# A four-layer float32 network on one core: the streamed 256-column tiles are read in another order, in pieces of 64 bytes

## The reference

```python
for layer in range(DEPTH):                      # 2 layers
    mixer = hgrn_gmlp_mixer if layer % 2 == 0 else mla_moba_mixer
    x = x + mixer(x, *mixer_params[layer])
    x = x + peer_ffn(x, *ffn_params[layer])
...
def peer_ffn(x, norm_ffn, w_query, sub_keys, expert_down, expert_up):
    # per token: 8 heads, each the top 16 of 128 x 128 = 16384 experts
    u = jnp.take(expert_down, idx, axis=0)
    act = jax.nn.gelu(jnp.einsum('btd,bthkd->bthk', xi, u))
    v_sel = jnp.take(expert_up, idx, axis=0)
    return jnp.einsum('bthk,bthkd->btd', g * act, v_sel)
```

## Time and profile before

| | |
|---|---|
| time, median of 3 runs | 3422.84 us (3422.46 to 3425.61) |
| the profiled execution's own time | 3413.89 us |
| its span | 3412.2 us |
| PE busy / weight loads busy | 91% / 88% of the span |
| DVE, ACT, POOL busy | 63%, 46%, 18% |
| mean granted TensorE clock | 0.95 of 2.4 GHz |
| matmul records | 25,254 |

### The profile page before, as it was taken

The page is one execution under the profiler, slowest core; times in us unless marked ns, Lnnn a source line. Parts: engine busy times, 40 slices in busy tenths (PEclk is TensorE's granted clock), DMA queues, the critical chain, the costliest instruction groups (busy, mean ns, idle before and its releaser), DMA issues. The chain is left out here.

```text
span 3412.2 us, 66107 instructions
## 1 busy us (share of the span) xinstructions
PE 3119.0 (91%) x25254; PEld 3013.7 (88%) x25254; DVE 2148.7 (63%) x3339; ACT 1571.3 (46%) x2653; POOL 609.7 (18%) x478
## 2 busy tenths in 40 slices
PE   8789999999998588999999997999987699899798
PEld 7689999999997488999999997999975689899697
DVE  4659698789864658888856775332255555454654
ACT  4244566644453444466645454222155244443343
POOL 0119700023321017900022222000010100000000
PEclk9889999999998699999999998999997699999899
DMA  5145544488884134544479893222150145455353
GB/s 173 53 155 172 181 145 143 152 276 299 309 303 124 41 124 161 179 160 144 145 241 314 309 311 132 96 98 93 61 164 11 50 136 185 143 186 163 124 191 123
DMA packets 178899, 560.66 MB, mean 164 GB/s; under 512 B 22480, under 2 KB 31440, under 8 KB 178144
## 3 DMA queue, kind: packets, MB, share of 16 engines
q1 hardware_dynamic: 178784, 559.21, 49.2%
HBM read 558.10 MB, written 1.05 MB: 164 GB/s over the span
## 5 line engine op out<-in xcount | busy, mean ns | idle before, releaser
L228 ACT ACTIVATE peer_e_hi<-peer_raw 128x1024 fp32r<-128x1024 f32 x512 | 539.3, 1054 | 355.6 <-PE peer_e_s L1180 178.0
L232 DVE TENSOR_TENSOR peer_e_lo<-peer_raw,peer_e_hi 128x1024 fp32r<-128x1024 f32 x416 | 516.8, 1244 | 275.9 <-ACT peer_e_hi L228 275.5
L232 DVE TENSOR_TENSOR ffn_lo<-ffn_raw,ffn_hi 128x1024 fp32r<-128x1024 f32 x260 | 318.6, 1227 | 499.9 <-ACT ffn_hi L228 499.9
L228 ACT ACTIVATE ffn_hi<-ffn_raw 128x1024 fp32r<-128x1024 f32 x264 | 279.6, 1061 | 546.0 <-PE ffn_acc L2007 343.1
L1226 PE MATMUL peer_e_o<-x_normed,peer_e_hi 128*128 128x256 f32 x2048 | 482.3, 278 | 13.5 <-ACT peer_e_hi L228 9.9
L1228 PE MATMUL peer_e_o<-x_normed,peer_e_hi 128*128 128x256 f32 x2048 | 481.6, 278 | 0.0
L1226 PEld LDWEIGHTS peer_e_o<-x_normed,peer_e_hi 128*128 128x128 f32 x2048 | 387.0, 189 | 14.3 <-ACT peer_e_hi L228 10.3
L232 POOL TENSOR_TENSOR x_normed<-peer_e_h,x_normed 128x256 fp32r<-128x256 f32 x256 | 207.1, 809 | 1038.1 <-ACT x_normed L228 1038.1
L1228 PEld LDWEIGHTS peer_e_o<-x_normed,peer_e_hi 128*128 128x128 f32 x2048 | 387.2, 189 | 0.0
L1998 PE MATMUL ffn_acc<-x_normed,ffn_hi 128*128 128x256 f32 x1408 | 354.9, 283 | 20.8 <-DVE x_normed L318 18.2
L1999 PE MATMUL ffn_acc<-x_normed,ffn_hi 128*128 128x256 f32 x1408 | 351.3, 281 | 0.0
(11 more groups left out here) (580 smaller groups left out, 7391.1 us busy)
## 6 DMA issues: line engine op xcount, KB each, us to landing
peer_raw<-in_l_down SPq DMA_DIRECT2D x256, 512.0 KB, 3.3
peer_raw<-in_l_up SPq DMA_DIRECT2D x256, 512.0 KB, 4.8
ffn_raw<-in_ffn_wi SPq DMA_DIRECT2D x176, 512.0 KB, 3.5
peer_ring<-in_w_mod SPq DMA_DIRECT2D x144, 512.0 KB, 5.2
ffn_raw<-in_ffn_wo SPq DMA_DIRECT2D x88, 512.0 KB, 3.4
l_in_raw<-in_l_w_in SPq DMA_DIRECT2D x39, 512.0 KB, 3.8
peer_q_raw<-in_l_peer_w_query SPq DMA_DIRECT2D x32, 512.0 KB, 4.0
wg_in_raw<-in_w_in SPq DMA_DIRECT2D x26, 512.0 KB, 4.1
```

Source lines behind the costliest of these rows:

```text
L228: return act.activation(hi, v, ACT.Copy)
L232: return eng.tensor_tensor(lo, v, hi.bitcast(F32), ALU.subtract)
```

## The change

In the four places above the streamed operand and the result get another access pattern over the same 256 elements. `striding` cuts the row into two halves of 128 elements (512 bytes) and each half into 8 pieces of 16 elements (64 bytes), and goes through piece 0 of the first half, piece 0 of the second half, piece 1 of the first, piece 1 of the second, and so on: each piece is followed by the one 512 bytes further. The result is written to PSUM in the same order, so that every element lands where it did. Weights, tiles, their places, waits and all instructions of the other engines stay as they were: each engine's program has as many rows after as before. The operand of each changed matmul goes from 128x256 to 128x8x2x16. The fp32 matmuls, form "t" and the recurrences' matmuls keep their patterns.

```diff
--- before.py
+++ after.py
@@ -92,6 +92,19 @@
     tile = padded(nc, stack, name, shape, dt, LINE)[0]
     stack.enter_context(nc.sbuf_tensor(f"{name}_after", [P, (LINE - MOVED) // 4], F32))
     return tile
+
+
+PIECE = 16
+
+
+def striding(a):
...
+    names = " ".join("abc"[:len(a.shape) - 2])
+    return a.rearrange(f"p {names} (two l e) -> p {names} l two e", two=2, e=PIECE)
 
 
 class Stage:
@@ -230,6 +243,11 @@
 
 def cut_lo(eng, lo, v, hi):
     return eng.tensor_tensor(lo, v, hi.bitcast(F32), ALU.subtract)
+
+
+def stream(pe, out, w, x, start, stop, lax=True):
+
+    return pe.matmul(striding(out), w, striding(x), start=start, stop=stop, skip_group_check=lax)
 
 
 def multiply(pe, out, w_hi, w_lo, x_hi, x_lo, start, stop, lax=False):
@@ -534,8 +552,9 @@
                             m = min(P, blk.width - j * P)
                             js = slice(j * P, j * P + m)
 
-                            mm = multiply(pe, acc[0:m, b % 2, j * T:(j + 1) * T], wh[:, c - c0, js],
-                                          wl[:, c - c0, js], xh, xl, c == 0 and j % 2 == 0, end, lax=True)
+                            mm = multiply(pe, striding(acc[0:m, b % 2, j * T:(j + 1) * T]), wh[:, c - c0, js],
+                                          wl[:, c - c0, js], striding(xh), striding(xl), c == 0 and j % 2 == 0, end,
+                                          lax=True)
                 mm.then_inc(product, 1)
 
         def tiles(b):
@@ -1173,11 +1192,11 @@
                 out = s_banks[k]
                 for c in range(DC):
                     w = hi[:, k % 2, c * P:(c + 1) * P]
-                    pe.matmul(out, w, K.xp[:, 0, c], start=c == 0, stop=False)
-                    pe.matmul(out, w, K.xp[:, 1, c], start=False, stop=False)
+                    stream(pe, out, w, K.xp[:, 0, c], c == 0, False, False)
+                    stream(pe, out, w, K.xp[:, 1, c], False, False, False)
                 pe.wait_ge(lo_sem, n + (1 - before))
                 for c in range(DC):
-                    mm = pe.matmul(out, lo[:, k % 2, c * P:(c + 1) * P], K.xp[:, 0, c], start=False, stop=c == DC - 1)
+                    mm = stream(pe, out, lo[:, k % 2, c * P:(c + 1) * P], K.xp[:, 0, c], False, c == DC - 1, False)
                 mm.then_inc(product, 1)
 
             for k in range(RAWS):
@@ -1223,13 +1242,11 @@
                 pe.wait_ge(lo_h, n + 1)
                 for c in range(DC):
                     w = hi[:, k % 2, c * P:(c + 1) * P]
-                    pe.matmul(o_ps[:, c], w, h_hi[:, k % 2], start=first and c % 2 == 0, stop=False,
-                              skip_group_check=True)
-                    pe.matmul(o_ps[:, c], w, h_lo[:, k % 2], start=False, stop=False, skip_group_check=True)
+                    stream(pe, o_ps[:, c], w, h_hi[:, k % 2], first and c % 2 == 0, False)
+                    stream(pe, o_ps[:, c], w, h_lo[:, k % 2], False, False)
                 pe.wait_ge(lo_up, n + 1)
                 for c in range(DC):
-                    mm = pe.matmul(o_ps[:, c], lo[:, k % 2, c * P:(c + 1) * P], h_hi[:, k % 2], start=False,
-                                   stop=False, skip_group_check=True)
+                    mm = stream(pe, o_ps[:, c], lo[:, k % 2, c * P:(c + 1) * P], h_hi[:, k % 2], False, False)
                 mm.then_inc(out_sum, 1)
 
             pe.wait_ge(weighted, BATCHES)
@@ -1995,8 +2012,8 @@
                             norms[s].wait_chunk(pe, c)
                         at = out[:, s * T:(s + 1) * T]
 
-                        pe.matmul(at, w, x.pair[:, 0, c], start=c == 0 and s == 0, stop=False, skip_group_check=True)
-                        pe.matmul(at, w, x.pair[:, 1, c], start=False, stop=False, skip_group_check=True)
+                        stream(pe, at, w, x.pair[:, 0, c], c == 0 and s == 0, False)
+                        stream(pe, at, w, x.pair[:, 1, c], False, False)
                 if made:
                     pe.wait_ge(lo_1, unit)
                 else:
@@ -2004,8 +2021,7 @@
                 for c in range(DC):
                     w = lo[:, j, c * P:(c + 1) * P]
                     for s, x in enumerate(streams):
-                        mm = pe.matmul(out[:, s * T:(s + 1) * T], w, x.pair[:, 0, c], start=False,
-                                       stop=c == DC - 1, skip_group_check=True)
+                        mm = stream(pe, out[:, s * T:(s + 1) * T], w, x.pair[:, 0, c], False, c == DC - 1)
                 mm.then_inc(product, 1)
 
             for k in range(2):
@@ -2024,14 +2040,12 @@
                 for c in range(DC):
                     w = hi[:, k, c * P:(c + 1) * P]
                     for s in range(n_s):
-                        pe.matmul(out_ps(s, c), w, gs(0, s), start=start and c % 2 == 0, stop=False,
-                                  skip_group_check=True)
-                        pe.matmul(out_ps(s, c), w, gs(1, s), start=False, stop=False, skip_group_check=True)
+                        stream(pe, out_ps(s, c), w, gs(0, s), start and c % 2 == 0, False)
+                        stream(pe, out_ps(s, c), w, gs(1, s), False, False)
                 pe.wait_ge(lo_2, f + 1)
                 for c in range(DC):
                     for s in range(n_s):
-                        mm = pe.matmul(out_ps(s, c), lo[:, k, c * P:(c + 1) * P], gs(0, s), start=False,
-                                       stop=False, skip_group_check=True)
+                        mm = stream(pe, out_ps(s, c), lo[:, k, c * P:(c + 1) * P], gs(0, s), False, False)
                 mm.then_inc(out_sum, 1)
 
             if n_s == 2:
```

## The result

| | before | after |
|---|---|---|
| time, median (range, runs) | 3422.65 us (3407.66 to 3425.61, 4) | 3531.86 us (3524.66 to 3535.18, 4) |
| the profiled execution's own time / span | 3413.89 / 3412.2 us | 3529.34 / 3527.6 us |

The ratio is 1.0325, 95% interval 1.0291 to 1.036: the change makes the kernel 109 us slower, where 3393 us was predicted. The first row of the page answers to the earlier trace rows: the counts are the same, PE is busy for 127 us more and its weight loads for 130, and DVE, ACT and POOL for no more than before.

A forecast was written before the change was run, and what follows sets the result against it. PE was taken as the bound, a chain of some 22,000 matmuls at 113.3 ns; 3413.9 less 22 us of long beat gives 3392, predicted as 3393 (chance 0.40), range 3310 to 3482.

The forecast's parts named there:

- Cost of the pattern: Step on going from piece to piece in changed matmuls: bounds 0 and 6.7 ns a matmul, 0 taken from strided row L837.
- A price per piece: Slower rival: at full rate each jump costs up to 0.42 ns, 6.7 a matmul, 134 us, giving 3526; chance 0.17.
- short beat: The faster of two paces a stage of 256-column matmuls keeps: 113.3 ns a matmul, 6.7 above its columns.
- Order against the weights: Step: row and weights keep pace through 512 bytes, 192 apart, so overtaking and the long beat end, saving 22 us.
- long beat: The slower pace of a stage, 117.8 ns a matmul, taken to be row and weights in each other's way.
- The 6.7 ns of the short beat: Step: the streamed row's excess over its 106.7 ns of columns, taken to stay unchanged.
- Short beat shortened too: Faster rival: the new order removes 4.0 ns a matmul, 80 us more, 3312, or 3346 if weight loads bound; chance 0.17.
- No effect: Rival: the beats come from something order doesn't touch, and fall anew; 3423, between 3405 and 3440; chance 0.18.
- Weights and row stay together: Slower rival: row and weights, at one pace, meet in every piece; long beat everywhere, 68 us, 3482; chance 0.08.
- Who else sets the pace: Step: POOL paces 96 score units, hiding up to 15 ns a matmul; DVE has 0.39 us room in routed scores; 20,040 matmuls count.
- The count: Number of matmuls whose pattern changes: 20,208 in PEER and SwiGLU and 2,136 in `project`, 22,344.
- The rule of the Trainium skill: Quoted against the change: any non-contiguous pattern slows matmuls significantly; by it the slow rival would happen.

The follow-up runs named there:

- f1: Changed kernel reading 64-byte pieces 0, 5, 10, 15 four times over, in plain-row order modulo 256 bytes, results written in a row: 3417.54 us.
- e9: Changed kernel with pieces of 32 bytes instead of 64, 32 of them: 3591.15 us.
- e3: Changed kernel with pieces of 128 bytes instead of 64, 8 of them: 3492.84 us.
- e10: Changed kernel (64-byte pieces, 512 bytes on) with rows 64 instead of 192 bytes past the weights: 3535.66 us.
- e8: Kernel before, rows contiguous, with rows 64 instead of 192 bytes past the weights: 3489.28 us.
- e11: Kernel before, rows contiguous, with rows 320 instead of 192 bytes past the weights: 3480.03 us.
- e13: Kernel before, rows contiguous, with rows 384 instead of 192 bytes past the weights: 3504.35 us.
- f3: Kernel before, contiguous, set to 224 bytes; only `ffn_g` and context rows lie 224 past the weights, `x_normed` stays at 192: 3441.57 us.
- f5: Kernel before, contiguous, set to 160 bytes; `ffn_g` and context rows lie 160 past the weights, `x_normed` 128: 3505.67 us.
- e4: Changed kernel with pieces of 256 bytes instead of 64, 4 of them, one profiled execution: 3419.16 us.
- f6: Changed kernel with pieces of 256 bytes, each followed by the one 512 further, timed against the kernel before: 3420.11 against 3431.84 us, ratio 0.9971.
- e2: Changed kernel with the streamed operand read contiguously again and only the result written in pieces: 3435.02 us.

## Why the prediction was wrong, point by point

- **The step that failed** is *Cost of the pattern*, "I take 0, the only strided row in the trace". It measured 6.7 ns per matmul, exactly the upper bound worked out there (0.42 ns for each of 16 pieces), and the rival *A price per piece* came out: 3526 against 3529.3 of the profiled execution. L837 misled since it ran at half the columns per ns, as the text itself warned. Its pieces also ascend through the row, so that their places modulo 256 bytes come in the order that f1 shows to be free; at half rate this can't be told from the other reason.
- **The rival's size was right, its mechanism wrong.** It said each jump costs. f1 makes 16 jumps for nothing, 32 jumps cost 10.0 and 8 cost 5.5 ns (e9, e3). What costs, against the short beat, is to leave the order of a plain row modulo 256 bytes.
- ***Order against the weights***: no stage of the changed kernel has the long beat, as predicted, but the cure costs more than the illness, 120.0 against 117.8, and the gain of 22 us is not seen. That nobody overtakes any more isn't shown: "192 bytes ahead" was said to be what keeps them apart, yet e10 has the same 120.0 at 64. That row and weights meet is borne out (moving either alone changes the pitch: e8, e11, e13, f3 to f5), with the period 256 bytes and not the 512 of the prediction; that the long beat is one overtaking the other is not shown.
- ***The 6.7 ns of the short beat*** I left as they are; where the order modulo 256 bytes is kept they do stay (f1, e4, f6). *Short beat shortened too* has no support: no kernel had a pitch under 113.3 in a changed stage.
- ***No effect*** and ***Weights and row stay together*** would have shown beats mixed as before, or 117.8 everywhere. The latter is what the contiguous row does at 64 bytes (e8), which 3489 us against the rival's 3482 fits; it isn't what the change did.
- ***Who else sets the pace***: POOL's slack of 0.37 us a unit was to cover up to 15 ns a matmul. It covered half: 3.09 became 3.17 us, 7.7 of 15 us came through. POOL's passes were no longer (2,873 ns against 2,903), it waited longer for ACT (11.4 against 7.0 us idle in 120), in the first section's row. ACT in turn waited for PE to free its tiles, for 70.0 us of these 120 and for 68.7 before. That the slack so was one of the sum and not of each handover is argued from this. In the routed scores DVE's room did suffice, and PE's 0.10 us a unit came through whole.
- **The count** of matmuls holds: 22,344 x 6.7, less the 22 and 8 us of the first section, is 120 for 115 measured.
- **The rule of the Trainium skill** that spoke against the change (PSUM — Partial Sum Buffer, Specifications (TRN2)) had the direction of the result. Its place is another: e2 puts nothing of the price on PSUM.

Open stays: why the period is 256 bytes, and whether rows in pieces meet the weights' reads as contiguous rows do or pay something of their own, since no kernel streamed them past weights that aren't loaded anew; why stages fall into one beat or the other at 192 bytes; and why steps of 128 bytes cost 8.0 ns.

## What to carry to other kernels

A price that the trace can't show at full rate has to be bounded and then chosen by its worst plausible end when the same trace shows that the engine it falls on is the bound: here 0.07 ns a piece turned the gain into a loss, and the bound that was named was the price. If a streamed row has to be read in another order, keep the order of places modulo 256 bytes (pieces of 256 bytes, or 64-byte pieces whose places follow each other as in a plain row; both were tried at 192 bytes alone); and try the distance of row and weights as a number, since the seven settings beside 192 bytes gave 3420 to 3525 us. Read in the source what such a setting moves: here it moved the weights, and two of the seven were rounded to distances that others had. Slack of an engine read from a window's busy time is not slack of each handover.

## What the runs showed of the hardware

- A 256-column fp32r matmul, streamed contiguously, took 113.3 to 120.0 ns by how far its row lay from the weights modulo 256 bytes (before, e8, e13, f3 to f5); the earlier trace rows had shown two of these values. Moving the weights alone changed it, and so did moving the row alone.
- Read in pieces of 64 bytes it took 113.3 or 117.8 ns with the order modulo 256 kept (f1) and 120.0 with one place revisited throughout (f2), at equal columns, pieces and jumps, 192 bytes past the weights.
- Writing PSUM in 16 pieces of 64 bytes cost nothing (e2, 113.0 and 117.6 ns by the windows, the beats of before).
- In cycles of 2.4 GHz the 120.0 ns lie 16 above the short beat (one for each 64 bytes), the 123.3 ns of 32-byte pieces 24, and the 118.8 ns of 128-byte pieces 13.
